# High and low half of the activations in one 512-column matmul, in three output stages of a float32 transformer kernel

## The reference, cut to what matters

```python
x = x + 0.5 * swiglu_2(rmsnorm_2(x, norm_ffn1), ffn1_gate, ffn1_up, ffn1_down)
...
merged = jax.nn.sigmoid(g_a) * (y_a @ w_up_a) + jax.nn.sigmoid(g_b) * (y_b @ w_up_b)
x = x + merged @ w_out
x = x + 0.5 * swiglu_2(rmsnorm_2(x, norm_ffn2), ffn2_gate, ffn2_up, ffn2_down)
```

## Time and profile before

| what | value |
|---|---|
| time, median of 3 runs | 2403.37 us (2401.61 to 2404.49) |
| the profiled execution's own time | 2402.99 us |
| span of the profiled execution (first to last instruction) | 2401.1 us |
| mean granted TensorE clock | 0.994 |
| TensorE busy, matmuls | 2328.5 us, 97% of the span |
| GpSimd / VectorE / ScalarE busy | 55% / 62% / 38% of the span |

### The profile page before, as it was taken

The page is one execution under the profiler, slowest core; times in us unless marked ns, Lnnn a source line. Parts: engine busy times, 40 slices in busy tenths (PEclk is TensorE's granted clock), DMA queues, the critical chain, the costliest instruction groups (busy, mean ns, idle before and its releaser), DMA issues.

```text
span 2401.1 us, 36091 instructions
## 1 busy us (share of the span) xinstructions
PE 2328.5 (97%) x14528; PEld 2074.6 (86%) x14528; DVE 1496.5 (62%) x2323; ACT 915.7 (38%) x1466; POOL 1332.2 (55%) x700
## 2 busy tenths in 40 slices
PE   7999999999989999999999998899999999999998
PEld 5888888777688888889888897789999999999998
DVE  8888597666578985977664126577527614534661
ACT  4222223455443222233222235554444444545443
POOL 3455465222234554664444443278878887468886
PEclk9999999999999999999999999999999999999999
DMA  6554353211025453534553322145545564245554
GB/s 269 193 179 172 136 211 100 71 54 62 27 80 193 170 180 136 202 119 173 176 194 111 97 93 71 45 158 185 178 155 189 179 193 158 96 146 185 182 179 136
DMA packets 97508, 350.09 MB, mean 146 GB/s; under 512 B 10944, under 2 KB 10944, under 8 KB 96960
## 3 DMA queue, kind: packets, MB, share of 16 engines
q1 hardware_dynamic: 97344, 347.81, 42.9%
HBM read 346.71 MB, written 1.05 MB: 145 GB/s over the span
## 4 chain that ended last, share of the span: by engine, by line
PE 59%; DVE 6%; issue 3%; ACT 2%; DMA 1%; POOL 1%; DVEq 0%; SPq 0%; ACTq 0%
PE psum L1562 19%; PE psum L1566 19%; PE psum L1563 19%; DVE psum L1123 2%; PE psum L1911 1%; POOL w_lo L770 1%; PE psum L1883 1%; ACT w_hi L790 1%; DVE psum L1203 0%; DVE h L1209 0%; PE psum L1891 0%; DVE u_lo L1420 0%; DVE pcomb L1393 0%; DVE stat L1478 0%; DMA w_raw<-in_ffn_in 0%
## 5 line engine op out<-in xcount | busy, mean ns | idle before, releaser
L770 POOL TENSOR_TENSOR w_lo<-w_raw,w_hi 128x1024 fp32r<-128x1024 f32 (+3 forms) x696 | 1332.0, 1936 | 1052.1 <-ACT w_hi L790 1051.4
L1562 PE MATMUL psum<-u_hi,w_hi 128*128 128x256 f32 (+2 forms) x2912 | 973.4, 334 | 9.8 <-POOL w_lo L770 6.2
L1566 PE MATMUL psum<-u_lo,w_hi 128*128 128x256 f32 (+2 forms) x2912 | 949.6, 326 | 3.5 <-DVE u_lo L1195 2.2
L1563 PE MATMUL psum<-u_hi,w_lo 128*128 128x256 f32 (+2 forms) x2912 | 947.6, 325 | 0.0
L790 ACT ACTIVATE w_hi<-w_raw 128x1024 fp32r<-128x1024 f32 (+1 forms) x522 | 534.0, 1031 | 501.0 <-PE psum L1566 383.8
L1562 PEld LDWEIGHTS psum<-u_hi,w_hi 128*128 128x128 f32 x2912 | 555.2, 191 | 77.4 <-issue 25.7
L1566 PEld LDWEIGHTS psum<-u_lo,w_hi 128*128 128x128 f32 x2912 | 554.7, 190 | 52.4 <-DVE u_lo L1195 4.7
L1563 PEld LDWEIGHTS psum<-u_hi,w_lo 128*128 128x128 f32 x2912 | 555.5, 191 | 45.7 <-issue 3.4
L1562 PE MATMUL psum<-gu_hi,w_hi 128*128 128x256 f32 (+1 forms) x1188 | 381.0, 321 | 6.3 <-DVE y L1222 6.2
L1563 PE MATMUL psum<-gu_hi,w_lo 128*128 128x256 f32 (+1 forms) x1188 | 379.5, 319 | 0.0
L1566 PE MATMUL psum<-gu_lo,w_hi 128*128 128x256 f32 (+1 forms) x1188 | 379.3, 319 | 0.0
(11 more groups left out here) (173 smaller groups left out, 1970.3 us busy)
## 6 DMA issues: line engine op xcount, KB each, us to landing
w_raw<-in_ffn_in SPq DMA_DIRECT2D x264, 512.0 KB, 3.5
w_raw<-in_ffn_out SPq DMA_DIRECT2D x96, 448.0 KB, 3.4
w_raw<-in_ffn_out SPq DMA_DIRECT2D x48, 512.0 KB, 3.6
ada_hi<-in_ada_w SPq DMA_DIRECT2D x44, 512.0 KB, 5.2
ada_lo<-in_ada_w SPq DMA_DIRECT2D x44, 512.0 KB, 5.1
ada_out<-in_ada_w SPq DMA_DIRECT2D x40, 512.0 KB, 4.3
w_raw<-in_b_qkv SPq DMA_DIRECT2D x30, 512.0 KB, 3.5
w_raw<-in_da_in SPq DMA_DIRECT2D x24, 512.0 KB, 3.5
```

The costliest lines, as they stand in the source:

```text
L770: last = pool.tensor_tensor(w_lo[:, slot, w], w_raw[:, slot, w], w_hi[:, slot, w].bitcast(F32), ALU.subtract)
L1562: mm(out, w_hi[:, slot, w], x_hi, start=start and n == 0, stop=False)
L1563: mm(out, w_lo[:, slot, w], x_hi, start=False, stop=False)
L1566: last = mm(out, w_hi[:, slot, w], x_lo, start=False, stop=stop and n == len(ks) - 1)
```

## The change

The high and low activations get one tensor each (`gu_both`, `mg_both`) with the low part behind the high part; the old names are slices of it, so the places in memory stay. In the output stages of the last layer a new function `side_by_side` takes the place of `blocks`: for each k one matmul streams high and low activations (two stretches of 256 columns, one from each half of the tensor) under `w_hi` into a whole bank of 512 columns, and a second one streams the high activations under `w_lo` into the first half. VectorE adds the first half of the bank to `h`, waits for that on a new semaphore `h_part`, and adds the second half.

```diff
-    gu_hi, gu_lo = take("gu_hi", [FCH, TOK], F32R), take("gu_lo", [FCH, TOK], F32R)
+    gu_both = take("gu_both", [2, FCH, TOK], F32R)
+    gu_hi, gu_lo = gu_both[:, 0, :, :], gu_both[:, 1, :, :]
...
-    mg_hi, mg_lo = take("mg_hi", [CH, SEQ], F32R), take("mg_lo", [CH, SEQ], F32R)
+    mg_both = take("mg_both", [2, CH, SEQ], F32R)
+    mg_hi, mg_lo = mg_both[:, 0, :, :], mg_both[:, 1, :, :]
...
                     dve.wait_ge(*piece_end(b, i))
-                    vec.scalar_tensor_tensor(out=h[:, j, tok], in0=psum[:, bank, tok], scalar=weight,
+                    vec.scalar_tensor_tensor(out=h[:, j, tok], in0=psum[:, bank, 0:SEQ], scalar=weight,
+                                             in1=h[:, j, tok], op0=ALU.mult, op1=ALU.add).then_inc(h_part, 1)
+                    dve.wait_ge(h_part, CH * (b["part"]) + j + 1)
+                    vec.scalar_tensor_tensor(out=h[:, j, tok], in0=psum[:, bank, SEQ:2 * SEQ], scalar=weight,
                                              in1=h[:, j, tok], op0=ALU.mult, op1=ALU.add).then_inc(h_ready, 1)
...
+        def side_by_side(slot, bank, moving, ks, start, stop, ready):
+
+            for n, k in enumerate(ks):
+                if ready is not None:
+                    ready(k)
+                w = slice(n * 128, (n + 1) * 128)
+                both = moving(k)
+                mm(psum[:, bank, :].rearrange("p (a b) -> p a b", a=2), w_hi[:, slot, w], both, start=start and n == 0, stop=False)
+                last = mm(psum[:, bank, 0:SEQ], w_lo[:, slot, w], both[:, 0, :], start=False, stop=stop and n == len(ks) - 1)
+            return last
...
-                        last = blocks(slot, psum[:, bank, tok], moving(tok), range(at, k1), first=at - k0,
-                                      start=at == 0, stop=ends, ready=None if i else ready)
+                        if b["layer"] is None:
+                            last = side_by_side(slot, bank, (lambda k: gu_both[:, :, k, LAT]) if b["kind"] == "ffn" else
+                                                (lambda k: mg_both[:, :, k, :]), range(k0, k1), k0 == 0, ends, None if i else ready)
+                        else:
+                            last = blocks(slot, psum[:, bank, tok], moving(tok), range(at, k1), first=at - k0,
+                                          start=at == 0, stop=ends, ready=None if i else ready)
```

More of the change, by code:

```diff
@@ L480, in build @@
     lat_done = sem("lat_done")
+    h_part = sem("h_part")
     ln_done, rstd_h_ready, rstd_y_ready = sem("ln_done"), sem("rstd_h_ready"), sem("rstd_y_ready")
```

## The result

| what | before | changed |
|---|---|---|
| time, median (14 runs each) | 2402.63 us (2398.53 to 2406.17) | 2408.16 us (2403.18 to 2412.18) |
| ratio, 95% interval | | 1.0021 (1.0013 to 1.0028) |
| profiled execution: its own time, span | 2402.99, 2401.1 us | 2405.68, 2403.8 us |

The forecast was 2398.4 us with a range to 2402.0 us; the time lies 6 us above the range, on the side that had a chance of 0.07.

A forecast was written before the change was run, and what follows sets the result against it. The prediction took TensorE's matmul starts to bound the changed stages. It summed -5.55 us for matmuls, +0.45 for the tail and +0.09 for `b2`'s first piece to -5.0 us: 2398.4 us from a median of 2403.37, range 2396.2 to 2402.0.

The forecast's parts named there:

- At the two seams to the next sub-block the last `u_lo` comes 0.45 us later: Behind the first two changed stages, the later `u_lo` still precedes TensorE's chunk 7; 2.2 us of cover remain, no cost.
- Lost in the mixer's body: Early in `b2`, shifted VectorE work meets GpSimd's long case; 2.5 us of stall reach TensorE, 2400.9 us, chance 0.08.
- Slower: In the changed stages, the 512-column matmul streams more slowly from two places; at two starts 2409.4 us, chance 0.07.
- The matmuls' term: In the three changed stages, 416 chunks each save one weight load and start, 0.0133 us, 5.55 us in all.
- The fixed part of a start: Each weight load and matmul carries 0.0133 us over its columns' streaming time, the same at 256 and 512 columns.
- the free jump: The jump between the two stretches of the 512-column operand was taken to cost nothing, with 0.0133 us kept for the range.
- their cover within a stage: Within a stage, 10.8 us more VectorE work is covered by its 4.9 us average wait for TensorE before each add.
- the tail: At the kernel's end nothing covers the second add: `hacc`, `h_sum`, `final` and the store move by 0.45 us.
- no wait for GpSimd inside the stages: In the changed stages GpSimd's weight preparation keeps up; its margin of about 0.4 us a tile shrinks by 0.1.

The follow-up runs named there:

- GpSimd's wait on before: Kernel before, with GpSimd waiting for the last `u_lo` before the fourth weight tile of the two sub-blocks behind changed stages: 2403.16 us, ratio 0.9999.
- before with the later request: Kernel before, with a 150-column VectorE copy ahead of chunk 6's `u_lo` at the first seam, so it is asked for later: 2403.18 us, ratio 1.0000.
- piece 7 alone with two adds: Changed kernel, in the first changed stage pieces 0 to 6 have one add (low halves left out), the last has two: 2397.85 us, ratio 0.9974.
- `u_lo` between the adds: Changed kernel, with VectorE doing the previous piece's sum of squares and `u_lo` between first and second add: 2398.88 us, ratio 0.9979.
- GpSimd's wait on the changed kernel: Changed kernel, with GpSimd waiting for the last `u_lo` before the fourth weight tile of the two following sub-blocks: 2397.69 us, ratio 0.9975.
- the two with matmuls grouped: Changed kernel, GpSimd waiting for the last `u_lo`, each tile's 512-column matmuls first: 2398.10 us; also excepting `b2`'s first piece, `hacc` between last-stage adds: 2396.50 us.
- the kernel with whole tiles: Changed kernel, with GpSimd making the first weight tiles behind the changed stages in one 1024-column operation instead of four: 2400.45 us, ratio 0.9984.
- The contiguous kernel: Changed kernel, with high and low activations of each chunk side by side, so the 512-column matmul reads one stretch: 2407.65 us, ratio 1.0013.

## Why the prediction was wrong

**The step that failed** is "At the two seams to the next sub-block the last `u_lo` comes 0.45 us later ... 2.6 us of cover stay 2.2. ... Covered too." It moved `u_lo` by 0.45 us with its duration kept, and checked that only against TensorE. What the 0.46 us did was to change which GpSimd operation the `u_lo` operations meet: with one add chunk 5's starts ahead of the run of 24, which begins as it ends; with two it falls on the start of the run, and the next one, of chunk 6, was held until that run had ended, for 9.34 us instead of 0.65. Cost +7.46 us, of which 6.0 are a wait of TensorE and the rest fits its lower clock. The row that could have warned is the earlier trace rows, 24 operations without a gap, read only for GpSimd's own pace.

**The rival "Lost in the mixer's body"** named the mechanism (VectorE's work moves against GpSimd's), but at another place, with 2.5 us and a chance of 0.08. Its bound was the 4.25 us of a pair in the earlier trace rows; the single `u_lo` at the seam took 9.34. The mixer's own wait of 0.8 us did not change. **The rival "Slower"** had a time near the measured one, 2409.4 us, but that is luck: its cause, a wide matmul that streams more slowly from two places, did not occur.

**The matmuls' term was mis-sized.** -0.0133 us for each of 416 chunks was -0.0067 as measured (0.3600 to 0.3533), so -2.8 us instead of -5.55. The fixed part of a start was right for matmuls among their like, and so was the free jump; the price of alternating between 512 and 256 columns was missing from the sum, and no row of before has such a sequence. Adds are 7.775 and 2.827 us apart, not 7.63 and 2.77. By the forecast's own terms with this one corrected the change would have brought -2.2 us, inside what cannot be told from nothing.

**Right by the profile:** the adds (0.42 us each, 0.46 apart) and their cover within a stage; the tail, +0.52 where 0.45 was forecast, with `h_sum` waiting 1.3 us instead of 0.8; no wait for GpSimd inside the stages. The end of the changed kernel, all in order of time for VectorE, then TensorE, as in the earlier trace rows:

```profile
2393.95 0.42 DVE L1345 SCALAR_TENSOR_TENSOR h<-psum,h 128x256 f32<-128x256 f32 x1 [6.56 <-PE psum L1583]
2394.41 0.42 DVE L1348 SCALAR_TENSOR_TENSOR h<-psum,h 128x256 f32<-128x256 f32 x1
2394.75 0.41 DVE L1179 TENSOR_TENSOR sq<-psum,sq 128x256 f32<-128x256 f32 x1
```

```profile
2395.22 0.70 PE L1616 MATMUL psum<-sq,ones 128*128 128x256 f32 x2 [1.31 <-DVE sq L1179]
```

**Shown and not shown.** Shown: the stall is at the seam, arises only from both halves of the change together, and goes with a wait of GpSimd or another order on VectorE, and with it the loss.

What starts it is shown only in part. In six of the sixteen traces with quarter tiles chunk 5's `u_lo` starts 0.46 us ahead of the run, which begins as it ends (before, the wide matmuls without second add, GpSimd's wait on before, before with the later request, piece 7 alone with two adds, `u_lo` between the adds), and none of them has the stall. In the other ten it starts with the run or up to 0.20 us into it: six stall. Of the four others, one (GpSimd's wait on the changed kernel) can't tell, since its run ends one operation after the request; its 1.11 us are no longer than the 1.12 us of before with the later request. The three others are before with the second add (1.03 us at 1970.24 us, its next pair 1.86 us) and the two with matmuls grouped. So the meeting is not enough. That it is needed rests on few traces, because it also shifts the operations of the run, and no run moved one without the other.

A rival for what else it takes is where in a GpSimd operation chunk 6's `u_lo` is asked for. In the six that stall it is 0.60 us (four), 0.12 and 0.14 us behind the start of one; in the three that meet the run and don't stall it is 0.05 us (before with the second add) and 0.53 us (the grouped ones, whose shorter pieces bring the request 0.1 us sooner). By itself this is not enough either: 0.61 us in before with the later request, and 0.11 us at the second seam of before (2201.51 us), gave no stall. Whether it is this moment or the order of the matmuls that spares the grouped kernels, no run separates. GpSimd's pace is no cause: the first twelve operations of the run, up to about the request, take 8.60 to 8.62 us in the traces that stall and 8.47 to 8.79 us in the others. Only all 24 differ, 16.83 to 16.86 us against 17.15 to 17.32, for a GpSimd operation beside which a `u_lo` gets its turn takes 0.9 us instead of 0.7. Why GpSimd gives VectorE no turn for so long stays open.

Open too is a matter of size. From the start of the last layer's first changed stage on, the traces of the kernels without a stall (second add out, GpSimd's wait, piece 7 alone with two adds) are only 2.6 to 2.7 us shorter than before's, while their medians are 5 to 6 us lower. So that these medians lie near the forecast's -5.0 us does not confirm its sum. The medians of most kernels with the stall are lower too than their traces say, by 2 to 5 us. From that start on, the four traces with alternating wide matmuls and no wait at the seam take 484.5 to 484.6 us and the four with the matmuls of before 486.9 to 487.7; what scatters lies ahead of it. The stage starts at 1913.5 to 1914.8 us in the four traces with the matmuls of before and at 1908.2 to 1915.8 us in the thirteen with wide ones, 1912.4 on average. So a part of the difference may arise ahead of the stages; one trace for each kernel can't show it, nor how often an execution stalls.

## What to carry to other kernels

Where VectorE and GpSimd both work from SBUF, an operation that is moved by half a microsecond has no fixed duration: look which operation of the other engine it will meet, above all a run without gaps, and count the wait as the length of the run and not of one operation. If the consumer is near, end such a run with a wait for the operation that is urgent, or queue the urgent operation ahead of the one that can wait. And a matmul's price is that of its sequence: equal column counts next to each other are the cheaper order, here by 0.09 us for a piece of 22 pairs, if nothing has to wait for it.

## What the runs showed of the hardware

**A run without gaps can hold VectorE to its end.** Usually a `u_lo` (two operands in SBUF) waits for one GpSimd operation: 2.69 us instead of 0.47 when it starts together with one of 1024 columns, 1.03 with one of a quarter tile, 2.6 to 2.7 in the kernel with whole tiles. The Trainium skill says so in "SBUF — State Buffer", section "SBUF: two separate sides": the two engines share a port pair, whichever starts first holds it for its whole instruction, and the other blocks. If the engine that waits came next, the `u_lo` asked for at 1974.85 us would by that rule have got its turn within one quarter-tile operation, 0.7 us, and nothing would have reached TensorE. It was held for 9.34 us, over thirteen of them (9.34 / 0.70), and for 9.1 to 9.8 us in six traces of the seventeen in all; each time it ended 0.28 us behind the run. The measurement decides: the engine that waits does not always come next, and blocking can last for many operations, each of which started later than the one that waits.

**A two-stretch operand is free.** 512 columns from two places and from one gave the same 7.775 and 2.827 us for a piece, and in a row of wide matmuls the two-stretch ones came down to the 0.2267 us of the contiguous ones in the earlier trace rows.

**Alternating 512 and 256 columns costs 0.0067 us for a pair**, 0.3533 us where the like matmuls in a row would take 0.3467. Grouped by tile, 0.02 us for each tile are left, in the first five wide matmuls behind the change.

**An idle stretch of 6.0 us costs more than itself:** the granted clock fell to 0.52, and the next 3 us of matmuls ran at 0.21 us for 256 columns, before it was back at 1.00. After the same wait of 6.0 us the slow stretch lasted some 5 us in three other traces, and the way from stage to stage cost 8.7 to 8.9 us instead of 7.5 to 7.6. The contiguous kernel, by windows, with the columns of the windows around the stall above:

```profile
1985.70:1988.70 3.00, 2.92 (x12) 2.83 (x13) 0.43 (x2) 0.00 (x0) 0.00 (x0) 0.50 0.03 8
1988.70:1991.70 3.00, 3.00 (x15) 2.73 (x14) 0.60 (x2) 0.83 (x2) 0.00 (x0) 0.57 0.94 339
```
